# A relative-bias table made ahead of a product, and the masks of a chunked scan loaded and applied earlier

## The reference

```
dist = t - key
bias = rel_bias[rel_bucket(max(dist, 0))]        # 32 buckets, 8 heads; masked where dist < 0
logits = q . k * NSA_HEAD_DIM ** -0.5 + bias
```

## Time and profile before

| | |
|---|---|
| profiled execution | 3457.58 us, span 3455.8 us |
| TensorE busy | 3027.0 us (88% of the span), mean granted clock 0.904 |
| VectorE, ScalarE, GpSimd busy | 1536.1, 1083.2, 57.9 us |
| HBM read / written | 213.87 MB / 19.09 MB |
| the features stage | about 921 to 1023 us |
| the scan | 1033.84 to about 1410 us |
| the values' product to `cmp_k` | 2135.72 to 2188.49 us |

### The profile page before, as it was taken

One profiled execution on the slowest core, in us unless ns is written; L12 is line 12 of the kernel. 1 busy time (PEld: TensorE's weight loads), 2 busy tenths in 40 slices (PEclk: granted clock), 3 DMA queues, 4 the chain that ended last, 5 costly groups with the idle time before them and its releaser, 6 DMA issues. The chain is left out here.

```text
span 3455.8 us, 54108 instructions
## 1 busy us (share of the span) xinstructions
PE 3027.0 (88%) x23264; PEld 2340.3 (68%) x23264; DVE 1536.1 (44%) x2546; ACT 1083.2 (31%) x1962; POOL 57.9 (2%) x80
## 2 busy tenths in 40 slices
PE   7799889989868888888899998798767899999997
PEld 3488656877747877446788776456455787778876
DVE  5523356354463343655444324355353434455522
ACT  5411357232243222212322222462240332332222
POOL 0000000000001111000000000000000000000000
PEclk9899999999859999698899998689875999989998
DMA  8511100123041111201233222202100222223321
GB/s 269 139 55 55 35 1 26 49 85 110 11 173 28 40 40 28 75 19 49 79 98 92 88 79 75 81 1 68 31 4 13 86 92 86 79 66 93 92 90 63
DMA packets 232560, 236.98 MB, mean 69 GB/s; under 512 B 28040, under 2 KB 205704, under 8 KB 232257
## 3 DMA queue, kind: packets, MB, share of 16 engines
q1 hardware_dynamic: 232018, 232.33, 22.2%
q10 hardware_dynamic: 304, 1.18, 0.1%
HBM read 213.87 MB, written 19.09 MB: 67 GB/s over the span
## 5 line engine op out<-in xcount | busy, mean ns | idle before, releaser
L201 DVE TENSOR_TENSOR second_w_low<-second_w_raw,second_w_high 128x1024 fp32r<-128x1024 f32 (+1 forms) x228 | 272.5, 1197 | 533.6 <-ACT second_w_high L197 533.5
L197 ACT CAST second_w_high<-second_w_raw 128x1024 fp32r<-128x1024 f32 (+1 forms) x228 | 233.6, 1024 | 719.4 <-PE ffn_in_acc L222 256.5
L220 PE MATMUL ffn_in_acc<-ffn_h_high,second_w_high 128*128 128x512 f32 x704 | 282.7, 402 | 14.5 <-DVE ffn_h_low L578 14.5
L222 PE MATMUL ffn_in_acc<-ffn_h_high,second_w_low 128*128 128x512 f32 x704 | 284.4, 404 | 0.0
L221 PE MATMUL ffn_in_acc<-ffn_h_low,second_w_high 128*128 128x512 f32 x704 | 281.1, 399 | 0.0
L201 DVE TENSOR_TENSOR first_w_low<-first_w_raw,first_w_high 128x1024 fp32r<-128x1024 f32 x115 | 140.2, 1223 | 264.2 <-ACT first_w_high L197 263.8
L197 ACT CAST first_w_high<-first_w_raw 128x1024 fp32r<-128x1024 f32 x115 | 120.0, 1046 | 230.9 <-PE attn_in_acc L222 80.2
L220 PEld LDWEIGHTS ffn_in_acc<-ffn_h_high,second_w_high 128*128 128x128 f32 x704 | 134.4, 191 | 49.1 <-issue 18.0
L221 PEld LDWEIGHTS ffn_in_acc<-ffn_h_low,second_w_high 128*128 128x128 f32 x704 | 134.5, 191 | 34.2 <-issue 0.5
L220 PE MATMUL attn_in_acc<-attn_h_high,first_w_high 128*128 128x256 f32 (+1 forms) x416 | 143.9, 346 | 14.4 <-DVE attn_h_low L323 14.4
L222 PEld LDWEIGHTS ffn_in_acc<-ffn_h_high,second_w_low 128*128 128x128 f32 x704 | 134.4, 191 | 31.4
(11 more groups left out here) (757 smaller groups left out, 6534.5 us busy)
## 6 DMA issues: line engine op xcount, KB each, us to landing
second_w_raw<-in_ffn_w_gate SPq DMA_DIRECT2D x44, 512.0 KB, 3.8
second_w_raw<-in_ffn_w_up SPq DMA_DIRECT2D x44, 512.0 KB, 3.8
second_w_raw<-in_ffn_w_down SPq DMA_DIRECT2D x40, 512.0 KB, 3.5
first_w_raw<-in_rec_w_in SPq DMA_DIRECT2D x33, 512.0 KB, 3.9
first_w_raw<-in_attn_ada_w SPq DMA_DIRECT2D x24, 512.0 KB, 4.7
first_w_raw<-in_rec_ada_w SPq DMA_DIRECT2D x24, 512.0 KB, 4.9
second_w_raw<-in_w_in SPq DMA_DIRECT2D x24, 512.0 KB, 3.9
second_w_raw<-in_w_branch_gate SPq DMA_DIRECT2D x24, 512.0 KB, 3.6
```

Source lines behind the costliest of these rows:

```text
L197: act.copy(self.view(self.high[b % self.splits], b), self.view(self.raw[b % self.bufs], b)).then_inc(self.high_done, 1)
L201: dve.tensor_tensor(self.view(self.low[b % self.splits], b), self.view(self.raw[b % self.bufs], b), self.view(self.high[b % self.splits], ...
L220: pe.matmul(out, sh, mh, start=(first and j == 0), stop=False)
L222: ins = pe.matmul(out, sl, mh, start=False, stop=(last and j == len(parts) - 1))
```

## The change

Two edits. In the mixer, `spread_line` and `rel_bias_rows` now stand ahead of the values' product, which was ahead of them. In the recurrent layer the constant `chunk` is loaded with the gates' weights, ahead of the features stage, into a tile that lives until the scan has ended; the semaphore of its own is gone. VectorE makes the diagonal `diag_t` itself, from PSUM, with a mask that is the product of the two masks (`near`, made once for both directions), behind each `gram_b`; GpSimd only makes `off_t` from it. `gram_k` is read after both.

```diff
@@ rwkv_gate_loads
+    loads.start(chunk[:], d["c_chunk"])
@@ rwkv_scan, marks
-RWKV_DVE = Marks("gram0", "gram1", "step4_0", ...
+RWKV_DVE = Marks("diag0", "diag1", "gram0", "gram1", "step4_0", ...
-RWKV_POOL = Marks("diag0", "off0", "diag1", "off1", "first0", "first1")
+RWKV_POOL = Marks("off0", "off1", "first0", "first1")
@@ SyncE, TensorE
-            sp.dma_start(chunk[:], d["c_chunk"]).then_inc(masks, 16)
-            pe.wait_ge(masks, 16)
@@ flip
-                    pe.wait_ge(pool_done, RWKV_POOL(n, f"diag{h}"))
+                    pe.wait_ge(dve_done, RWKV_DVE(n, f"diag{h}"))
@@ GpSimd
-            pool.wait_ge(masks, 16)
-                    pool.wait_ge(dve_done, RWKV_DVE(n, f"gram{h}"))
-                    pool.tensor_tensor(dt[:, h], gb[dr][:, h, :, 0, :], each_head(same), ALU.mult).then_inc(pool_done, 1)
-                    pool.wait_ge(pool_done, RWKV_POOL(n, f"diag{h}"))
+                    pool.wait_ge(dve_done, RWKV_DVE(n, f"diag{h}"))
                     pool.tensor_tensor(et[:, h], gb[dr][:, h, :, 0, :], dt[:, h], ALU.subtract).then_inc(pool_done, 1)
@@ VectorE
-            dve.wait_ge(masks, 16)
+            for dr in range(2):
+                ins = dve.tensor_tensor(near[:, dr, :], chunk[:, 2 * dr, :], same, ALU.mult)
+            chain.link(ins)
...
+                dve.wait_ge(pe_done, RWKV_PE(n, "gram1"))
                 for h in range(2):
-                    dve.wait_ge(pe_done, RWKV_PE(n, "gram1"))
-                    dve.tensor_tensor(gb[dr][:, h].rearrange("p i a t -> p i (a t)"),
-                                      ps[2 * h][:].rearrange("p (i t) -> p i t", t=P), mask, ALU.mult)
+                    of = ps[2 * h][:].rearrange("p (i t) -> p i t", t=P)
+                    dve.tensor_tensor(gb[dr][:, h].rearrange("p i a t -> p i (a t)"), of, mask, ALU.mult)
+                    dve.tensor_tensor(dt[:, h], of[:, :, 0:CH], near[:, dr:dr + 1, :].broadcast_to([P, PAIRS, CH]),
+                                      ALU.mult).then_inc(dve_done, 1)
+                for h in range(2):
                     dve.tensor_tensor(gk[dr][:, h].rearrange("p i a t -> p i (a t)"),
@@ mixer
-            linear_tokens(nc, "nsa_v", w, *u, S, ...)
             spread_line()
             rows = ...
             rel_bias_rows(nc, d, relative, ...)
+            linear_tokens(nc, "nsa_v", w, *u, S, ...)
@@ rec_layer
+                chunk = tokens.enter_context(nc.sbuf_tensor("rec_chunk", [P, 6, CH], F32, side="right"))
```

More of the change, by code:

```diff
@@ L1544, with rwkv_gate_loads @@
 CUM = CH + 1
-def rwkv_gate_loads(nc, d, stack, w0_at):
+def rwkv_gate_loads(nc, d, stack, w0_at, chunk):
     loads = Ahead(nc, stack, "rwkv_up")
@@ L1851, with rwkv_scan @@
                  "eight0", "eight1", "inverse0", "inverse1", "solved0", "solved1", "way0", "way1")
-RWKV_DVE = Marks("gram0", "gram1", "step4_0", "step4_1", "step8_0", "step8_1", "step16_0", "step16_1",
+RWKV_DVE = Marks("diag0", "diag1", "gram0", "gram1", "step4_0", "step4_1", "step8_0", "step8_1", "step16_0", "step16_1",
                  "z1_0", "z1_1", "z2_0", "z2_1", "z3_0", "z3_1")
-RWKV_POOL = Marks("diag0", "off0", "diag1", "off1", "first0", "first1")
+RWKV_POOL = Marks("off0", "off1", "first0", "first1")
 SCAN = Marks("sa0", "new0", "sa1", "new1")
-def rwkv_scan(nc, d, c, vt, ends, y, feats):
+def rwkv_scan(nc, d, c, vt, ends, y, feats, chunk):
     groups = [(dr, ((4, 5, 0, 1, 2, 3), (5, 4, 3, 2, 1, 0))[dr][step]) for step in range(6) for dr in range(2)]
@@ L1865, in rwkv_scan @@
     with Stage(nc, "rwkv") as st:
-        chunk = st.sb("chunk", [P, 6, CH])
         same, eye = chunk[:, 4, :], chunk[:, 5, :]
@@ L1875, in rwkv_scan @@
             "diag_t", "off_t", "diag", "inv", "value", "eight", "z"))
+        near = st.sb("near", [P, 2, CH])
         a2, a4, mh = (st.sb(n, [P, 2, 2, PAIRS, CH]) for n in ("square", "four", "inverse"))
@@ L1878, in rwkv_scan @@
         landed = [st.sem(f"landed{i}") for i in range(2)]
-        pe_done, act_done, dve_done, pool_done, scan_pe, scan_dve, out_pe, out_dve, cleared, own, masks = (
+        pe_done, act_done, dve_done, pool_done, scan_pe, scan_dve, out_pe, out_dve, cleared, own = (
             st.sem(x) for x in ("pe_done", "act_done", "dve_done", "pool_done", "scan_pe", "scan_dve", "out_pe",
-                                "out_dve", "cleared", "own", "masks"))
+                                "out_dve", "cleared", "own"))
         block = st.block()
@@ L3436, in mixer @@
                           update=update, column=column)
-            linear_tokens(nc, "nsa_v", w, *u, S, lambda e, b, t, ps: copy_on(e, nc, vs[:, t, :], ps[:, 0:256], column[:, t:t + 1]))
             spread_line()
@@ L3441, in mixer @@
             rel_bias_rows(nc, d, relative, [r.rearrange("p (h m) -> p h m", m=REL_KEYS) for r in rows])
+            linear_tokens(nc, "nsa_v", w, *u, S, lambda e, b, t, ps: copy_on(e, nc, vs[:, t, :], ps[:, 0:256], column[:, t:t + 1]))
             rows_to_tokens(nc, "nsa_gate_turn", gate_rows[:], gates, c["ident"])
@@ L3742, in rec_layer @@
                 feats = [tokens.enter_context(nc.sbuf_tensor("rec_first_feats", [P, 4, PAIRS, P], F32, side="right"))]
+                chunk = tokens.enter_context(nc.sbuf_tensor("rec_chunk", [P, 6, CH], F32, side="right"))
                 gates_kept = mid.enter_context(ExitStack())
-                gate_loads = rwkv_gate_loads(nc, d, gates_kept, v.where["w0_rows"][0])
+                gate_loads = rwkv_gate_loads(nc, d, gates_kept, v.where["w0_rows"][0], chunk)
                 rwkv_features(nc, "rwkv_feat", d, c, v, us, vt, v_feat[:], bonus, ends,
@@ L3748, in rec_layer @@
             scanned = sb("scanned", [P, 4, S], mid)
-            rwkv_scan(nc, d, c, vt, ends, scanned, feats)
+            rwkv_scan(nc, d, c, vt, ends, scanned, feats, chunk)
             tokens.close()
```

## The result

The changed kernel takes 3413.93 us (median of 4 runs, 3409.50 to 3422.27) against 3455.31 for the kernel before on the same chip: ratio 0.988, 95% interval 0.9853 to 0.9907. That is 41.4 us less; the forecast was 31.5 less (3426.1), with a range of 3409 to 3443. The profiled execution took 3409.88 (span 3408.1), 47.7 less than the profiled one of before.

| stretch | before | after | difference |
|---|---|---|---|
| features (first tile cleared to the scan's state cleared) | 109.9 | 104.8 | -5.1 |
| scan, to the first product of the late filters | 400.5 | 377.5 | -23.0 |
| late filters, to the output projection | 165.6 | 162.9 | -2.7 |
| sparse attention, from the start of the first stage's last L220 product to cmp_k | 54.6 | 37.6 | -17.0 |
| everything else | | | +0.1 |

The account below looks back on a forecast made before the run. TensorE was taken to wait for the bias table ahead of the flips, the masks at the scan's start and GpSimd's diagonal. -12.5 - 3.1 + 1.0 - 11.0 - 2.0 - 3.9 = -31.5 gives 3426.1 us, range 3416 to 3437 (8 in 10: 3409 to 3443).

Parts of the forecast that it names:

- rival B: Scan and flips: clock stays high, all seven falls in the scan go and flips run fast; 3415.1 us, chance 0.2.
- Part one, -12.5: Sparse attention: bias table spread, written and read ahead of the values' product, flips 12.5 us earlier; bounds 8.5 to 14.4.
- The same again gives 2155.95: Sparse attention: from the table's first read issue to the flips it stays 14.95 us, a gain of 12.5.
- so I take none: Flips in sparse attention: no gain counted from a higher clock, though 3.9 us more would go if high at once.
- Part two: -3.1: Scan's start: masks loaded ahead, so TensorE starts with the stage, 3.1 us gained.
- +1.0: Features' start: first product also waits for the masks' load on the shared semaphore, 0.6 to 1.4 us late.
- Part three, -11.0 for the groups: Scan: VectorE makes the diagonal, next product at +4.1 instead of +5.13 us; 1.0 gained in each of eleven groups.
- First group, -2.0: Scan's first group, without state update: squares start at +3.9 (full clock) or +4.8 (half) instead of +6.32; 2.0 us gained.
- Clock, -3.9: Scan: half of the five clock falls behind the flips' waits go, 1.57 us each; bounds -7.9 and 0.
- A: Scan: no gain per group, as second squares wait behind the first value, which needs gram_k; 3441.0 us, chance 0.12.
- C: Scan: GpSimd blocks VectorE's state update on the shared port, 4.0 us back; 3430.1 us, chance 0.1.
- D: Scan: pauses strewn through each group make the clock fall everywhere, slower; 3479.0 us at 5 us each, chance 0.03.

Follow-up runs that it names:

- experiment 8: Kernel before with 18 more TensorE products, result overwritten, in the wait for the bias table ahead of the flips: 3458.57 us, ratio 1.0007.
- experiments 6: Changed kernel with two more VectorE products, result unused, ahead of the scan's state update in every group: 3423.48 us, ratio 0.9908 to the kernel before.
- experiment 7: Changed kernel with the state update ahead of gram_k and TensorE's values, with ScalarE's copies of them, behind the squares: 3415.81 us, ratio 0.9895 to the kernel before.
- experiment 9: Changed kernel with VectorE's additions to the scan's output moved behind the corrections: 3403.21 us, ratio 0.9852 to the kernel before.
- experiment 5: Changed kernel again, no edit, profiled and timed beside its variants: 3415.19 us, ratio 0.9889 to the kernel before.

## Why the forecast was right, and where its sizes were off

The direction, the places and the mechanism of each part held; the sum was 10 us short. The measured 3413.9 lies outside the forecast's own 3416 to 3437 and inside 3409 to 3443 only because that range took rival B in. That it stands 1.2 us from B's 3415.1 is in part luck: of B's two gains only the flips came whole, and the rest was made up by three terms that were too small.

- **Part one, -12.5: measured -17.0 to -17.2.** Two steps were mis-sized. "The same again gives 2155.95": from the read's issue to the flips it was 12.9 us, not 14.95. The bound that took the small copy out of the way had 1.9 less, and the rows fit it (the copy, now alone, takes 4.8 us instead of 9.2), but no run moves the copy alone, so the cause is argued and not shown. The line's write took 0.5 us longer in this profile; the flips come 1.6 us earlier for both, 14.1 in all, close to the bound of 14.4. The weight loads issued right behind the table, which I feared would cost up to 4.0, show no such cost. The Trainium skill ("DMA: Bandwidth & Descriptors", Queues, rings and completion order) says descriptors of a queue start in ring order; by that rule I had 14.4 ready and took the old duration instead. The trace agrees, with 14.1. Second, "so I take none" for the clock: worth 3.0, and experiment 8 shows that the clock, not chance, makes the difference. The 3.9 named there was too much, since the first 14 rows take 6.28 us even at full clock. TensorE was still busy 2 us before the flips, which I had counted as 4 us of idleness. The product's own slow start (1.5 us) costs nothing in this profile, where the flips wait for the table. The load at 2135.72, taken for the values' product's own, is of cmp_k's weights; the product's first row is at 2135.77, which changes no term.
- **Part two: -3.1 was -3.2, +1.0 was +0.6 to +0.9.**
- **Part three, -11.0 for the groups: 1.14 each by the product's place, -12.5** (1.05 to 1.31 by the periods without a fall). The forecast of +4.1 for the next product was +3.98, since the read costs 0.33 instead of 0.40 and the sizes follow. That the state update is what it waits for is only half true: TensorE's queue ends at the same moment (experiments 6 and 7), which a reader of the trace could have added up: two flips and two values from +1.15 on. The waits ahead of the flips shrank further than the forecast's "about 1.1", to about 0.5 in all.
- **First group, -2.0:** squares at +3.72 behind the first gram instead of +6.32, -2.6; 0.9 more came ahead of that gram, from a clock that rose sooner.
- **Clock, -3.9:** three of seven falls went: all five behind the flips did, and the four left, where there had been two, stand behind another wait. The periods fell by 19.2: 2.6 in the first, ten times 1.14, which leaves 5.2 for the clock and for pauses that vary. In other pairs it is more: between the means of the five profiles with the old diagonal (333.9) and the four with the new one (311.2) it is 22.7, and 37 falls in five profiles stand against 13 in four, 7.4 against 3.3 each. The forecast counted 2.5 of the five falls behind the flips; all of those went, some others came behind the sixteenth step, and about four fewer at 1.57 make 6.3 us, an estimate.
- **Rivals.** A (no gain per group) is refuted by every period. B was right on the flips and half right on the scan, where all falls behind the flips went and four others stayed (two to four in the profiles with VectorE's diagonal and the output additions in their old place). C did not come: VectorE's state product took 0.42 us beside a waiting GpSimd (1166.59). D is out.
- **Not foreseen:** the features' -6 and the late filters' -2.7 in the profiled pair. The kernel before shows 104.4 and 109.9 us for the first by itself, and its unedited filters take 168.1 in experiment 8. Both vary with the granted clock in code that nobody changed. Whether the change also tips them a little is open: no run here holds the clock of those stages fixed.

## What to carry to other kernels

A transfer moved under a product is worth more than its wait if the engine behind it then starts busy rather than idle: count the slow clock behind the hole as part of the hole. When a wait is taken away, add up the queue of the engine that waited as well as the releaser's; here both end just ahead of +3.98, and a product made 0.9 us earlier by putting some of TensorE's own work behind it brought nothing. The next gain stood elsewhere in the same loop, where a late addition sat in VectorE's queue ahead of a step that TensorE waited for (12 us for moving it). And an unchanged stage that differs by 5 us between two profiles is compared with further profiles of the unchanged code before it is explained; one more can agree by chance, as the scan's 331.6 and 331.8 did.

## What the hardware showed that I had not expected

- A stage of 105 us varies by 5.5 us in one unchanged kernel with its granted clock (0.55 or 0.68 mean over its middle), while the total repeats: 3457.1 and 3457.58 us. Over all 14 profiles it lasts 100.8 to 109.9 us, and the unchanged scan 400.4 to 407.4 in four.
- 18 products brought the clock to 1.00 (0.50 in the window from 2148 to 2152, where they begin, 0.66 from 2152 to 2156, 1.00 from there), and the 14 rows behind them ran in 6.17 us instead of 9.29.
- VectorE and GpSimd can both lose. In experiment 7 the state product beside GpSimd's difference took 0.72 us instead of 0.42:
```profile
1168.72 0.72 DVE L2185 TENSOR_TENSOR rwkv_state<-rwkv_state,rec_ends 128x256 f32<-128x256 f32 x1
```
  In the kernel before it was GpSimd that lost (0.99 against 0.72). The Trainium skill ("SBUF — State Buffer", SBUF: two separate sides) has VectorE with two SBUF inputs and GpSimd share a port pair that the first taker keeps for its whole instruction. The trace agrees in that the one that started second was the slower in both cases (GpSimd started 0.02 us behind VectorE, VectorE 0.28 behind GpSimd). It lost 0.27 and 0.30 us, less than the 0.40 and 0.45 us for which the first was still at work.
- From the issue of the line's write to that of the read it was 1.78 to 1.80 us in eleven profiles and 2.29, 2.33 and 2.44 in three (both of the changed kernel, experiment 7), with the same 32 KB.
- Short waits decide where the clock can fall, but not whether it does. The falls behind the flips went with waits of 0.82 to 1.29 us, those behind the sixteenth step with one of 1.89 (experiment 9); but such waits stood in nearly every group, and falls behind them only in some, and in other ones from profile to profile. Each fall is worth 0.8 to 1.6 us beyond the wait itself (29.09 against 27.52 us in the earlier trace rows; 30.25 against 29.46 in neighbouring groups of experiment 5, both with the 1.89).
